# Seven half-block products instead of eight for the gate and up projections of a two-layer trunk

## What is computed

```python
gate, up = jnp.split(x @ lw['w_up'], 2, axis=-1)      # 1024 -> 2 x 2816
x = layer_norm(ALPHA * x + (jax.nn.silu(gate) * up) @ lw['w_down'], lw['ln2_g'], lw['ln2_b'])
```

## Time and profile before

| | us |
|---|---|
| median of 3 runs | 2097.69 |
| lowest, highest | 2095.34, 2098.29 |
| span of the profiled execution | 2097.1 |
| PE busy | 2072.3 |
| DVE busy | 1169.4 |
| ACT busy | 713.2 |

### The profile page before, as it was taken

The page is one execution under the profiler, slowest core; times in us unless marked ns, Lnnn a source line. Parts: engine busy times, 40 slices in busy tenths (PEclk is TensorE's granted clock), DMA queues, the critical chain, the costliest instruction groups (busy, mean ns, idle before and its releaser), DMA issues.

```text
span 2097.1 us, 38539 instructions
## 1 busy us (share of the span) xinstructions
PE 2072.3 (99%) x16020; PEld 1996.6 (95%) x16020; DVE 1169.4 (56%) x1886; ACT 713.2 (34%) x1152; POOL 81.3 (4%) x96
## 2 busy tenths in 40 slices
PE   7999999999999999999999999999999999999999
PEld 6899999898999999999998999989889999999998
DVE  5434645774377666654465365466724866566433
ACT  4232134444343232222343221354433433222232
POOL 1000000000011000000010000010000200000110
PEclk9999999999999999999999999999999999999999
DMA  5232222321132223223333222132213223323331
GB/s 171 78 77 58 61 54 64 93 62 51 51 101 81 85 85 90 83 81 93 86 92 83 78 59 76 40 93 59 63 34 93 84 81 90 90 80 88 84 90 54
DMA packets 287876, 163.45 MB, mean 78 GB/s; under 512 B 8984, under 2 KB 279552, under 8 KB 287744
## 3 DMA queue, kind: packets, MB, share of 16 engines
q1 hardware_dynamic: 283712, 152.07, 25.9%
q0 software_dynamic: 3552, 8.36, 1.3%
q10 hardware_dynamic: 480, 1.13, 0.2%
HBM read 156.86 MB, written 4.66 MB: 77 GB/s over the span
## 4 chain that ended last, share of the span: by engine, by line
PE 97%; DVE 1%; ACT 1%; issue 0%; DMA 0%; DVEq 0%; ACTq 0%
PE acc L696 50%; PE acc L682 27%; PE ring L718 4%; PE ring L802 2%; PE ring L956 2%; PE ring L975 1%; PE acc L718 1%; PE ring L964 1%; PE ring L1026 1%; PE ring L1008 1%; PE ring L1256 1%; PE ring L853 0%; PE ring L839 0%; PE ring L829 0%; PE ring L832 0%; PE acc L845 0%
## 5 line engine op out<-in xcount | busy, mean ns | idle before, releaser
L1388 ACT ACTIVATE whi<-raw 128x1024 fp32r<-128x1024 f32 (+6 forms) x340 | 312.0, 918 | 739.2 <-PE acc L696 404.0
L1970 DVE TENSOR_TENSOR wlo<-raw,whi 128x1024 fp32r<-128x1024 f32 (+6 forms) x340 | 355.0, 1046 | 299.7 <-ACT whi L1388 298.8
L696 PE MATMUL acc<-xh,whi 128*128 128x272 f32 x1376 | 310.7, 307 | 3.6 <-DVE xl L1970 3.4
L682 PE MATMUL acc<-xh,whi 128*128 128x274 f32 x1472 | 308.5, 290 | 0.0
L682 PE MATMUL acc<-xh,wlo 128*128 128x274 f32 x1472 | 305.9, 289 | 0.0
L682 PE MATMUL acc<-xl,whi 128*128 128x274 f32 x1472 | 305.5, 289 | 0.0
L696 PE MATMUL acc<-xh,wlo 128*128 128x272 f32 x1376 | 285.9, 289 | 0.0
L696 PE MATMUL acc<-xl,whi 128*128 128x272 f32 x1376 | 285.7, 289 | 0.0
L696 PEld LDWEIGHTS acc<-xh,whi 128*128 128x128 f32 x1376 | 218.2, 190 | 19.1 <-issue 14.4
L682 PEld LDWEIGHTS acc<-xh,whi 128*128 128x128 f32 x1472 | 232.2, 189 | 0.6
L682 PEld LDWEIGHTS acc<-xl,whi 128*128 128x128 f32 x1472 | 231.6, 189 | 0.0
(11 more groups left out here) (411 smaller groups left out, 3118.2 us busy)
## 6 DMA issues: line engine op xcount, KB each, us to landing
raw<-in_w_in_dram SPq DMA_DIRECT2D x104, 512.0 KB, 3.7
raw<-in_w_up_dram SPq DMA_DIRECT2D x88, 512.0 KB, 3.7
raw<-in_w_down_dram SPq DMA_DIRECT2D x32, 512.0 KB, 3.8
raw<-in_w_o_dram SPq DMA_DIRECT2D x16, 512.0 KB, 3.8
raw<-in_w_down_dram SPq DMA_DIRECT2D x16, 384.0 KB, 3.3
raw<-in_w_pc_dram SPq DMA_DIRECT2D x16, 256.0 KB, 2.8
raw<-in_w_pb_dram SPq DMA_DIRECT2D x16, 256.0 KB, 2.8
raw<-in_w_pa_dram SPq DMA_DIRECT2D x16, 256.0 KB, 2.8
```

What stands on the lines that cost most here:

```text
L682: last = pe.matmul(dst[:, at_:at_ + x1 - x0], wq[:, k * P:(k + 1) * P], x[:, k, x0:x1], start=k == 0 and q == 0, stop=k == KD - 1 and q == 2)
L696: last = pe.matmul(dst[:, b * 512:b * 512 + HALF], w[:, c:c + P], x[:, k0 + a, b * HALF:(b + 1) * HALF], start=start and a == 0 and q == 0 ...
L1388: return act.activation(dst, src, ACT.Copy)
L1970: return dve.tensor_tensor(out, a, b, op)
```

## The change

The first four f (8 units, `STD_F`) stay as they are. From the fifth on, a pair (gate and up unit of one f) is computed as one product of 2 x 2 blocks: x is cut into token halves 1, 2 and feature halves 1, 2 (`x11`, `x12`, `x21`, `x22`, each 4 k by 272 tokens), and so are the weights (w11 and w21 the gate's feature halves, w12 and w22 the up's). Strassen's scheme in its form with shared sums takes seven products of half blocks where the plain one takes eight:

- Four sums of x blocks (s3, s1, s2, s4), once a layer; four differences of weight blocks (t1 and t3 in one operation, t2, t4), for each pair. For all seven x blocks (`xb`) the high and low parts are made, and for all seven weight blocks of each pair, in eight slots six products ahead (`SLOTS`, `AHEAD`), four of them in the memory of `xh` and `xl`.
- For that x must be fully normalised before the pairs: `x_norm` and `x_gained` run during units 1 to 4 of the up phase, in operations of 1088 elements, and the residual later only multiplies by ALPHA.
- A product is 12 matmuls of 272 columns into one bank; three banks serve a pair (`pair_banks`, two sets in turn). Sums of products are formed by letting PE go on in a bank after ACT has copied its content out (`keep`), and by DVE (`pair_lin`). Then sigmoid, gate, h.
- h is kept whole (`hid`); its high and low parts are made in operations of two f at the end, in the last pair and after it, `hh` over the place of the x blocks and `hl` in place.
- The loops are gone: everything is written out. Loads of a pair's buffers wait until all seven low parts of the pair two before are done.

Core of the diff, cut:

```diff
+STD_F = 4
+PAIRS = KF - STD_F
+SLOTS, AHEAD = 8, 6
+PRODUCTS = ("x11_w11", "s3_t3", "s2_t2", "x12_w21", "s1_t1", "x22_t4", "s4_w22")
...
-    hh, hl = at_off("hh", 17408, [P, KF, T], F32R), at_off("hl", 65280, [P, KF, T], F32R)
+    hid = at_off("hid", 17408, [P, KF, T])
+    hh, hl = at_off("hh", 65280, [P, KF, T], F32R), at_off("hl", 17408, [P, KF, T], F32R)
+    xb = at_off("xb", 65280, [P, OF_PAIR, 2, 4 * HALF], F32R)
...
+        def pair_products(layer, p):
+            a, b, c = pair_banks(p)
...
+            for i, dst in enumerate((a, b, a, c, a, b, a)):
+                q = OF_PAIR * p + i
+                pe.wait_ge(*at("wt_lo", layer, q + 1))
+                if p == 0:
+                    pe.wait_ge(*at("xb_lo", layer, i + 1))
...
+                elif i in (2, 4, 5, 6):
+                    pe.wait_ge(*at("pr_kept", layer, 4 * p + {2: 1, 4: 3, 5: 2, 6: 4}[i]))
+                w1, w2 = weight_slot(q)
+                first = i in (0, 1, 3)
+                for k in range(4):
+                    for r, (w, part) in enumerate(((w1, 0), (w1, 1), (w2, 0))):
+                        last = pe.matmul(dst[:, 0:HALF], w[:, k * P:(k + 1) * P], block_of(i, part)[:, k, :],
+                                         start=first and k == 0 and r == 0, stop=k == 3 and r == 2, skip_group_check=True)
+                last.then_inc(*inc("pr_done"))
...
-            with pe.Fori(1, KF // 2) as i:
...
+            for p in range(PAIRS):
+                pair_products(l, p)
             for c in range(8):
                 for j, (k0, kn) in enumerate(DOWN):
...
                     if j == 0:
+                        if c < 2:
+                            pe.wait_ge(*at("pr_h", l, 2 * PAIRS))
+                            pe.wait_ge(*at("pr_lin", l, 3 * PAIRS))
                         dst = tile(f"dn{c}", l)
...
+        def h_hi(l, f):
+            for g in (f, f + 1):
+                if g < STD_F:
+                    act.wait_ge(*at("up_h", l, g + 1))
+                else:
+                    act.wait_ge(*at("pr_h", l, 2 * (g - STD_F) + 2))
+            act.wait_ge(*at("pr_done", l, OF_PAIR * (PAIRS - 1) + (f + 1) // 4 + 1))
+            copy(hh[:, f:f + 2, :], hid[:, f:f + 2, :]).then_inc(inc("h_hi", 2)[0], 2)
...
+            x_steps = {2: [(x_gained, 0), (x_gained, 1), (x_gained, 2), (x_gained, 3)], 3: [(x_gained, 4), (x_gained, 5)],
+                       4: [(x_gained, 6), (x_gained, 7), (block_hi, 0)], 5: [(block_hi, 1), (block_hi, 2)],
+                       6: [(block_hi, 3), (block_hi, 4)], 7: [(weight_hi, 0), (weight_hi, 1), (block_hi, 5), (block_hi, 6)]}
...
+            tail = {1: [(h_hi, 0), (h_hi, 2)], 2: [(h_hi, 4), (next_hi, U_DN)], 3: [(h_hi, 6)], 4: [(h_hi, 8), (h_hi, 10), (next_hi, U_DN + 1)],
+                    5: [(h_hi, 12)], 6: [(h_hi, 14), (h_hi, 16), (h_hi, 18), (h_hi, 20)]}
+            for p in range(PAIRS):
+                for i in range(OF_PAIR):
+                    if i in (0, 1, 2, 4):
+                        keep(l, p, (0, 1, 2, 4).index(i))
...
+                    q = OF_PAIR * p + i + AHEAD
+                    if q < OF_PAIR * PAIRS:
+                        weight_hi(l, q)
+                    else:
+                        for step, n in tail[i]:
...
+                    if i == 5:
+                        pair_sigmoid(l, p)
...
+            def x_norm(l, k):
+                tt(y[:, k:k + 2, :], y[:, k:k + 2, :], rs[:, :].unsqueeze(1).broadcast_to([P, 2, T]), ALU.mult).then_inc(inc("x_prod", 2)[0], 2)
+                dve.wait_ge(*at("x_prod", l, k + 2))
+                tt(y[:, k:k + 2, :], y[:, k:k + 2, :], tmp[:, :].unsqueeze(1).broadcast_to([P, 2, T]), ALU.add).then_inc(inc("x_norm", 2)[0], 2)
...
+            def pair_h(l, p):
+                f = STD_F + p
+                dve.wait_ge(*at("pr_sig", l, p + 1))
+                tt(gs[:, 0, :], gs[:, 0, :], gs[:, 1, :], ALU.mult).then_inc(*inc("pr_gate"))
+                dve.wait_ge(*at("pr_gate", l, p + 1))
+                dve.wait_ge(*at("pr_done", l, OF_PAIR * (p + 1)))
+                tt(hid[:, f, 0:HALF], gs[:, 0, 0:HALF], pair_banks(p)[0][:, 0:HALF], ALU.mult).then_inc(*inc("pr_h"))
+                tt(hid[:, f, HALF:T], gs[:, 0, HALF:T], hid[:, f, HALF:T], ALU.mult).then_inc(*inc("pr_h"))
...
+            x_steps = {1: [(x_norm, 0), (x_norm, 2)], 2: [(x_norm, 4)], 3: [(x_norm, 6)], 4: [(block_sums, B_S3), (block_sums, B_S1)],
+                       5: [(block_sums, B_S2), (block_sums, B_S4), (block_lo, 0)], 6: [(block_lo, 1), (block_lo, 2)],
+                       7: [(block_lo, 3), (block_lo, 4)]}
+            for j in range(2 * STD_F):
+                up_normalised(j, j // 2)
+                if j < 2 * STD_F - 2:
+                    lo_part(l, U_UP + j + 2)
+                elif j == 2 * STD_F - 2:
+                    for n in range(3):
+                        weight_sum(l, 0, n)
+                else:
+                    weight_lo(l, 0)
+                    weight_lo(l, 1)
+                up_out(j, j // 2)
+                for step, i in x_steps.get(j, ()):
+                    step(l, i)
+            for q in range(2, AHEAD):
+                weight_lo(l, q)
+                if q < 4:
+                    block_lo(l, q + 3)
...
+            tail = {1: [(h_lo, 0), (h_lo, 2)], 2: [(h_lo, 4)], 3: [(next_lo, U_DN), (h_lo, 6)], 4: [(h_lo, 8), (h_lo, 10)],
+                    5: [(h_lo, 12), (next_lo, U_DN + 1)], 6: [(h_lo, 14), (h_lo, 16), (h_lo, 18), (h_lo, 20)]}
+            for p in range(PAIRS):
+                for i in range(OF_PAIR):
+                    if i in (3, 4, 5):
+                        pair_lin(l, p, i - 3)
+                    if i == 6:
+                        pair_h(l, p)
+                    q = OF_PAIR * p + i + AHEAD
+                    if q < OF_PAIR * PAIRS:
+                        weight_lo(l, q)
+                    else:
+                        for step, n in tail[i]:
+                            step(l, n)
+                    if i < 3 and p + 1 < PAIRS:
+                        weight_sum(l, p + 1, i)
```

More of the change, by code:

```diff
@@ L483, in two, with weight_slot, weight_terms, raw_blocks @@
         return ap.rearrange("p (b c) -> p b c", b=2)
+    x_flat = [t[:, :, :].rearrange("p k t -> p (k t)") for t in (xgh, xgl)]
+    def weight_slot(q):
+        s = q % SLOTS
+        if s < 4:
+            return whi[s // 2][:, 512 * (s % 2):512 * (s % 2) + 512], wlo[s // 2][:, 512 * (s % 2):512 * (s % 2) + 512]
+        ap = x_flat[(s - 4) // 2][:, 1024 * (s % 2):1024 * (s % 2) + 1024]
+        return ap[:, 0:512], ap[:, 512:1024]
+    h_tail = hid[:, KF - 4:KF, :].rearrange("p k t -> p (k t)")
+    def weight_terms(p):
+        if p == 0:
+            return h_tail[:, 0:1024], h_tail[:, 1024:1536], h_tail[:, 1536:2048]
+        high, low = (t[:, 0:1024] for t in x_free)
+        return high, low[:, 0:512], low[:, 512:1024]
+    def raw_blocks(p):
+        g = (U_PAIRS + 2 * p) % RAW * SLOT
+        assert g in (0, 2 * SLOT)
+        return [raws[:, g + 512 * i:g + 512 * i + 512] for i in range(4)]
+    def weight_block(q):
+        p, i = divmod(q, OF_PAIR)
+        w11, w21, w12, w22 = raw_blocks(p)
+        t13, t2, t4 = weight_terms(p)
+        return (w11, t13[:, 512:1024], t2, w21, t13[:, 0:512], t4, w22)[i]
+    kept = [t[:, 1024 + HALF * i:1024 + HALF * (i + 1)] for i in range(2) for t in x_free]
+    def x_quarter(i, j):
+        return y[:, 4 * j:4 * j + 4, HALF * i:HALF * i + HALF]
+    def block_of(i, part):
+        return xb[:, i, part, :].rearrange("p (k t) -> p k t", k=4)
+    def block_sum(i):
+        return xs[:, i, 1, :].rearrange("p (k t) -> p k t", k=4)
+    def block_source(i):
+        name = PRODUCTS[i][:3]
+        return x_quarter(int(name[1]) - 1, int(name[2]) - 1) if name[0] == "x" else block_sum(i)
+    B_X11, B_S3, B_S2, B_X12, B_S1, B_X22, B_S4 = range(OF_PAIR)
+    def pair_banks(p):
+        if p % 2 == 0:
+            return bank[0], bank[1], bank[2]
+        t = (tile_at["up7"]) % 2
+        return bank[3], acc[t][:, 0:512], acc[t][:, 512:1024]
     def tile_freed(name, layer, i=0, per=0):
@@ L626, in _, with pair_read @@
                     load(l, U_WO + j, raw3(U_WO + j, KD, P), w_o[l, 4 * i + j], i, 4)
-            with sp.Fori(0, KF // 2) as i:
-                for j in range(4):
-                    load(l, U_UP + j, raw3(U_UP + j, KD, P), w_up[l, j % 2, 2 * i + j // 2], i, 4)
+            def pair_read(l, n):
+                p = (n - RAW - U_PAIRS) // 2
+                if 0 <= p < PAIRS:
+                    sp.wait_ge(*at("wt_lo", l, OF_PAIR * (p + 1)))
+                    passed(sp, "sp")
+                return not 0 <= p < PAIRS
+            for n in range(U_UP, U_DN):
+                f, j = divmod(n - U_UP, 2)
+                load(l, n, raw3(n, KD, P), w_up[l, j, f], first=pair_read(l, n))
             for c in range(8):
@@ new lines, in keep, with pair_sigmoid @@
+        def keep(l, p, n):
+            i = (0, 1, 2, 4)[n]
```

(37 more changed lines are left out.)

196 lines of the change are left out of this document (130 added, 66 removed).

## The result

The changed kernel takes 2082.81 us (median of 4 runs, 2079.81 to 2084.93) against 2097.69 us before: ratio 0.993, with a 95% interval of 0.9918 to 0.9943. The forecast was 2081.5 us. The profiled execution spans 2083.1 us, against 2097.1 before.

A forecast was written before the change was run, and what follows sets the result against it. PE, busy 99% of the span, was taken as the bound. Per layer 29.1 us gross, less 11.6 head, 7.9 tail and 1.5 clock, left 8.1; twice, 16.2, off 2097.7 gave 2081.5 us, range 2072 to 2095.

The forecast's parts named there:

- gross: Up units, per layer: PE's 218.6 us of removed units against 189.5 us of added pairs, a gain of 29.1 us.
- head: Before and in the first pair: PE waits 8.7 us for DVE, then 1.2 and 1.6 us more; 11.6 us lost.
- tail: Before the first down unit: PE waits 7.4 us for the last pair's h; with late copies 7.9 us lost.
- clock: After the tail's pause PE runs at about half clock for 3.3 us, costing 1.4 to 1.5 us a layer.
- I charge nothing for either: Pairs: twelve matmuls running to one bank, and bank changes, add no time; 0.12534 us a matmul.
- The rival of the bank's pace: Pairs: 0.1313 us a matmul in one bank, 9.0 us less gain a layer, 2099.5 us; chance 0.07.
- DVE in a pair: Pairs: DVE needs 9.7 us, including 0.3 waiting for the sigmoid, against PE's 10.53, so 0.8 us to spare.
- DVE becomes the bound: Pairs, head and tail: DVE operations cost 0.08 or 0.11 us more each, giving 2111.6 or 2131 us; chance 0.10 together.
- after the head's it costs nothing, as DVE sets the first pair: First pair: slow clock after the head's pause adds 0 us, because PE there runs behind DVE.
- 1.2 + 1.6 us: First pair: fifth product 1.2 us late behind DVE's low parts; copy before the seventh another 1.6 late on ACT.
- the count of products is what shows: Whole kernel: head and tail are hidden after all, gaining 29.1 us in each of two layers, 2039.5 us; chance 0.05.
- It needs DVE to be 18 us faster in 48: Condition set for hiding head and tail: DVE 18 us faster in 48; half of it would give 2060 us.

The follow-up runs named there:

- e4_thin: The changed kernel with the fifth and sixth product of each pair using only the last of four k (66 matmuls a pair, not 84): 2039.16 us.
- e1_banks: The changed kernel with the pairs' two bank sets exchanged, so the first down unit waits only for the pair before the last: 2072.16 us.
- e2_order: The changed kernel with high and low parts of h 10 to 13 and the second down weight moved behind the last pair's h: 2076.4 us.
- e3_no_norm: The changed kernel without the eight operations that normalise x for the products: 2079.88 us.
- e5_plus2: The changed kernel with two more DVE operations of 512 elements in 17 of the 18 pairs: 2086.24 us.
- e7_std5: The changed kernel with five plain f, weight and x sums prepared over the plain units, last pair on the other banks: 2069.28 us.
- e10_std5b: e7_std5 with the first two low parts of the weights written ahead of the last plain unit's evacuation: 2064.67 us.
- e9_std6f: e8_std6e with the split of h's parts 14 and 15 moved ahead of the last pair's evacuation: 2050.43 us.
- e8_std6e: The changed kernel with six plain f, banks exchanged, x sums spread wider, first two weights' low parts before the last plain evacuation: 2057.79 us.
- e6_plus4: The changed kernel with four more DVE operations of 512 elements in 17 of the 18 pairs: 2129.16 us.

## Why the prediction was right, point by point

**The place of the bound, the signs and the sum.** All of it held: matmuls 15588, PE idle ahead of the first product (7.4 forecast as 8.7) and ahead of the first down unit (7.1 for 7.4), the clock falling after the second, pairs of 10.6 us with DVE 90% busy. The gain was 8.0 us a layer for 8.1. That it came within 0.1 us is luck: the terms were off by up to 1.2 us, in both directions:

| term, us per layer | forecast | measured | from |
|---|---|---|---|
| gross | 29.1 | 27.9 | 0.1261 a matmul, not 0.12534 |
| head | -11.6 | -10.5 | first product 7.9 late, first pair 2.6 longer |
| tail | -7.9 | -7.6 | pause 7.1, and 0.5 before it |
| clock | -1.5 | -2.3 | 22 matmuls in 5.04 us |
| rest (down units) | 0 | +0.5 | 109.50 for 109.98; why is not shown |
| sum | 8.1 | 8.0 | |

**The pace.** "I charge nothing for either" was wrong by 0.0008 us a matmul: 12 matmuls in a row to one bank take 1.51 or 1.52 us. The rival of the bank's pace (0.1313) is ruled out by the same rows. The N/2.4 + 2.5 ns that the prediction cites from the Trainium skill, "TensorE: Matmul & The Clock Gate", Back-to-back issue gap, is there the gap of a matmul by itself; for a stream with weight loads, as here, the section gives other figures. The 0.1253 to 0.1264 us of the rows decide.

**DVE in a pair.** Forecast 9.7 us, measured 9.27 (e4_thin): the 0.3 us of waiting for the sigmoid was charged too high, since other work lies in it (0.1 is left in that chain), and the rest is a few hundredths an operation. The durations were right: 512 elements 0.69, the next start 0.60 later in the rows above (705.45, 706.05, 706.65). On this the rival "DVE becomes the bound" fell. The prediction gave this rival weight by a sentence of the Trainium skill. "VectorE: DVE Perf Modes", The DRAIN you can't avoid, says that the next operation does not start until the pipe empties, but it goes on to say that one that is not held starts earlier. The rows agree with the second sentence: each operation starts 0.08 to 0.09 us before the end that its predecessor's row gives, with waits between them that are satisfied.

**The head.** DVE was forecast to take 48.6 us up to the first weight (the terms add up to 48.4) and took 47.7, and "after the head's it costs nothing, as DVE sets the first pair" held, though PE's rows alone suggest otherwise. PE runs at half clock from 706.39 to about 710.9 and never waits for the fifth product. From 706.39 to 717.63 (0.36 us before 717.99) it makes 72 matmuls in 11.24 us, where 0.1261 each makes 9.08, so PE loses 2.2 us to the clock. But they are not on the path. The chain reaches the seventh product over DVE and ACT (start, us, what):

```profile
714.47 1.22 DVE xf L2170
...
716.30 0.61 DVE xf L2170
...
716.93 0.02 ACT whi L1510
...
717.47 0.39 ACT xf L1510
```

DVE works without a pause up to there, and its weight differences for the second pair set the high part on ACT, behind which the copy for the seventh product stands. The fifth product, whose result is copied, had ended at 715.95, 1.5 us before that copy. A PE at full clock would have waited longer for the same copy. The runs show it: in both layers of the change, e1_banks, e2_order and e3_no_norm the six products took 1.5 to 2.5 us longer than their 9.08, the wait ahead of the seventh was between 1.0 and 0.0, longest where the clock cost PE least, and the seventh started 11.6 us after the first each time. Only in the second layer of e5_plus2, where they took 2.7 us longer, did it start 0.2 us later. So the 1.2 + 1.6 us forecast for DVE and ACT are together the 2.6 measured. In the kernels with five plain f this cover is gone (no wait ahead of the seventh product), and there the fall of the clock at the head does cost time: the six products take 11.5 us (e7_std5) and 10.6 (e10_std5b), and the chain runs over PE.

**The tail.** "The first down unit waits for that h (its tile is the last pair's bank)" is shown by e1_banks; that h stands "behind low parts that don't need it" by e2_order. The clock stretch was longer than the one it was sized by: 4.8 us against 3.3.

**Rivals.** That the count of products is what shows (2039.5) was given 0.05. It didn't happen with this kernel, but e9_std6f gains 47 of those 58 us, by order, banks and two more plain f: "It needs DVE to be 18 us faster in 48" was too narrow. DVE need not be faster, if two more f, at 1.55 us each, hide its backlog.

## What to carry to other kernels

A cheaper method for the middle of a stage is paid for at its two ends: count the work that must be done before the first piece and after the last one, on the engine that does it, and leave as many pieces to the old method as hide that work (here two f for 3.1 us a layer, against 10 us of head). An engine at 90% beside the bound has a spare in time per piece that two added operations can use for next to nothing and four turn into a loss; find it by thinning the bound engine's work. At a seam, look for what stands in a queue ahead of the one result that the next stage waits for, and on which bank or buffer that stage starts. And a loss seen on one engine (here 2.2 us of slow clock at the head) counts only if the chain runs over that engine there.

## What the runs showed of the hardware

- The clock fell after pauses much shorter than the 7 us of the change: 1.84 us in e8_std6e, 1.9 in e1_banks and e10_std5b (0.67 and 0.75 in the five-microsecond windows there). In e7_std5 a pause of 1.90 us ahead of 905.49 left it at 1.00 in both layers, and with pauses of 0.2 and 0.3 (e9_std6f) it stayed at 1.00. So the length of a single pause doesn't decide alone; what else does was not tried.
- The half-clock stretch lasted 4.8 us after 7.1 us of pause, some 4.5 us after 7.4, some 3.1 us after 5.6 (e3_no_norm's head), and 3.3 us after 3.4 in the kernel before. PE loses half of it each time. A layer of the change had two, of which only the tail's cost time.
- The loss varies at the same pause: with 7.1 us ahead of the first down unit in four kernels, the first layer's down matmuls took, from the start of the first to that of the last, from 134.5 us (e3_no_norm) to 135.3 (e6_plus4), 135.1 in the change.
- The fall need not be there at once: in e8_std6e it came 1.1 us after PE had resumed.
- The time up to the first plain up unit scattered by 4.6 us between executions (654.5 to 659.1), with the same code ahead of it. Comparing spans alone would have credited e1_banks with 16.2 us, when its medians say 10.7.
